# Softmax steps of a decoder layer: value products and sample pieces moved between the scores and the weights' transposes, on TensorE

## The reference

```python
def block(args):                       # i: one block of 128 queries
    i, qn, qr = args
    s = jnp.einsum('bqhn,bkhn->bhqk', qn, k_nope) + jnp.einsum('bqhp,bkp->bhqk', qr, kr)
    s = s.astype(F32) * MLA_SCALE
    s = jnp.where(key_pos[None, :] <= q_pos[:, None], s, -jnp.inf)
    p = jax.nn.softmax(s, axis=-1).astype(v.dtype)
    return jnp.einsum('bhqk,bkhv->bqhv', p, v)
...
# samples
q_lat = jnp.einsum('bshn,rhn->bshr', q_nope, w_uk)
state = jnp.exp(gt)[..., None] * state + kt[..., None] * vt[..., None, :]
```

## Time and profile before

| | us |
|---|---|
| median of 3 runs | 735.47 (734.77 to 735.70) |
| the profiled execution, its own time | 736.7 |
| its span in the trace | 734.9 |
| the stretch of steps 4 to 49 in it | 168 (from 388 to 556) |

### The profile page before, as it was taken

How to read it: one execution, slowest core, us unless ns; L and a number is a source line. 1 busy time by engine, 2 the same in 40 slices (tenths; PEclk the granted TensorE clock), 3 DMA queues, 4 the chain that set the end, 5 groups by cost and what they waited for, 6 DMA issues and landing times.

```text
span 734.9 us, 16715 instructions
## 1 busy us (share of the span) xinstructions
PE 700.0 (95%) x7021; PEld 549.6 (75%) x7021; DVE 355.9 (48%) x775; ACT 326.7 (44%) x779; POOL 91.1 (12%) x140
## 2 busy tenths in 40 slices
PE   2899999999999999899899999999999999999995
PEld 1487878878789997677667766777677998678884
DVE  0455370030202025777675676667671112389967
ACT  1244660021202137767556666645675667502100
POOL 0000000000000011101124323232113442000000
PEclk9899999999999999999999999999999999999998
DMA  9987300302001001000010000202756884203332
GB/s 289 395 351 214 112 3 1 114 1 76 22 1 58 1 29 58 16 10 16 9 12 2 1 2 0 59 1 74 243 187 214 293 290 150 61 1 117 135 123 86
DMA packets 35013, 70.31 MB, mean 96 GB/s; under 512 B 6594, under 2 KB 17947, under 8 KB 33020
## 3 DMA queue, kind: packets, MB, share of 16 engines
q1 hardware_dynamic: 30602, 47.73, 20.1%
q0 software_dynamic: 3728, 20.97, 8.1%
q10 hardware_dynamic: 610, 0.55, 0.3%
HBM read 62.26 MB, written 6.07 MB: 93 GB/s over the span
## 4 chain that ended last, share of the span: by engine, by line
PE 90%; DVE 3%; ACT 2%; issue 1%; DMA 1%; another core or an unknown queue 1%; ACTq 1%; DVEq 0%
PE banks L2051 21%; PE banks L2247 8%; PE banks L2063 6%; PE banks L2377 5%; PE banks L2461 4%; PE banks L2481 3%; PE banks L2590 3%; PE banks L2592 3%; PE banks L2591 3%; PE banks L2072 2%; PE banks L2530 2%; PE banks L2549 2%; PE banks L2155 2%; PE banks L2573 2%; PE banks L2574 2%; PE banks L2580 2%
## 5 line engine op out<-in xcount | busy, mean ns | idle before, releaser
L1122 ACT ACTIVATE s_z<-banks 128x512 f32<-128x512 f32 (+3 forms) x40 | 19.6, 500 | 129.0 <-PE banks L2051 129.0
L2051 PE MATMUL banks<-s_w_parts,s_h_b 128*128 128x272 f32 (+3 forms) x328 | 68.2, 323 | 0.0
L1334 ACT ACTIVATE s_z<-banks 128x512 f32<-128x512 f32 (+2 forms) x88 | 41.3, 518 | 45.6 <-PE banks L2461 44.5
L1497 DVE COPY s_zs<-banks 8x512 f32<-8x512 f32 (+3 forms) x6 | 3.5, 576 | 118.5 <-PE banks L2025 118.5
L2051 PEld LDWEIGHTS banks<-s_w_parts,s_h_b 128*128 128x128 f32 x328 | 49.3, 189 | 4.6 <-issue 1.7
L1325 ACT ACTIVATE s_z<-banks,s_temps 128x896 f32<-128x896 f32 (+7 forms) x64 | 47.1, 741 | 11.0 <-DVE s_temps L1775 8.0
L2051 PE MATMUL banks<-s_w_parts,s_h_a 128*128 128x256 f32 (+2 forms) x256 | 49.8, 314 | 0.0
L2051 PE MATMUL banks<-s_z_r,s_h_b 128*128 128x512 f32 (+1 forms) x152 | 48.8, 387 | 0.0
L2461 PEld LDWEIGHTS banks<-s_ident,s_z 128*128 128x128 f32 x288 | 33.2, 141 | 11.7 <-issue 5.5
L2461 PE MATMUL banks<-s_ident,s_z 128*128 128x128 f32 x288 | 40.0, 275 | 1.3 <-DVE s_z L1791 1.2
L2051 PE MATMUL banks<-s_z_r,s_h_a 128*128 128x512 f32 x128 | 40.9, 395 | 0.0
(11 more groups left out here) (427 smaller groups left out, 1544.6 us busy)
## 6 DMA issues: line engine op xcount, KB each, us to landing
s_z<-in_w_ada SPq DMA_DIRECT2D x16, 512.0 KB, 12.2
s_temps<-in_w_in SPq DMA_DIRECT2D x3, 2048.0 KB, 7.7
s_x<-in_x_prompt SPq DMA_DIRECT2D x8, 512.0 KB, 12.0
s_z<-in_w_ada SPq DMA_DIRECT2D x1, 4096.0 KB, 13.9
s_kt<-in_w_out SPq DMA_DIRECT2D x8, 512.0 KB
s_temps<-in_x_prompt SPq DMA_DIRECT2D x8, 512.0 KB
out_y_prompt<-s_temps SPq DMA_DIRECT2D x7, 512.0 KB
s_temps<-in_w_in SPq DMA_DIRECT2D x2, 832.0 KB, 14.2
```

The source lines that it names most:

```text
L1334: nc.scalar.activation(PTb[r % 3][:, 4 * g:4 * g + n, :], banks[:, 4 + (groups(r) + g) % 2, 0:P * n].rearrange("p (j q) -> p j q", j=n), A ...
L2051: last = nc.tensor.matmul(banks[:, proj_bank(c, t), 0:WIDTH[c]], h_[half][:, k, n0:n0 + P], w_, start=(k == 0 and n == 0), stop=(k == KT - ...
```

## The change

In PE's loop the products and TAIL's piece now stand in front of `weights_turned(r)`. A piece at HEAD stays where it was. TAIL's projections and transposes of queries stay behind the turning. The products that stood ahead of the turning in step 48 still do. No instruction is added or taken away, no wait is changed, and no other engine's stream differs.

```diff
                             if s == len(STEPS):
                                 products(N_PAIRS_OF_HEADS - 2)
-                            weights_turned(r)
                             for p in range(N_PAIRS_OF_HEADS - 2):
                                 if last_step(p) == r - 1:
                                     products(p)
+                            if piece_at(s, TAIL):
+                                piece((s, TAIL))
+                            weights_turned(r)
                     if (s, place) in PROJECTED_AT:
                         bank_of_queries((s, place))
                         q_proj(*PROJECTED_AT[s, place])
                     if (s, place) in TURNED_AT:
                         bank_of_queries((s, place))
                         q_transpose(*TURNED_AT[s, place])
-                    if piece_at(s, place):
-                        piece((s, place))
+                    if place == HEAD and piece_at(s, HEAD):
+                        piece((s, HEAD))
```

## The result

The changed kernel takes 738.81 us (median of 6 runs, 738.12 to 741.70), the kernel before 735.14 (6 runs, 732.44 to 737.11). The ratio over the runs is 1.0062, with a 95% interval of 1.0044 to 1.0080: slower by 3.2 to 5.9 us. The two medians by themselves stand 3.67 us, or 0.50%, apart. The forecast was 739.0 us, range 737.0 to 741.6.

What follows compares the result with a forecast made beforehand. The prediction took PE to bound steps 4 to 49 (busy 166.1 of 168 us). Costs of 6.7 us less gains of 1.8 and 1.4 made +3.5 on the median 735.47: 739.0 us, range 737.0 to 741.6.

Steps and rivals of the forecast that it cites:

- three takers of bank 7: Steps 14/15, 20/21 and 23/24: PE work needing bank 7 waits for ACT's later copy, +1.1 us each, 3.3 together.
- q0: Step 11: q0 waits for ACT's later copy of the transpose of queries, seven transposes come behind it, +1.3 us.
- qlat: Step 29: qlat waits for ACT's copy of a transpose of queries, held behind delayed exponentials, +0.5 us.
- P27: Step 44: these products wait for ACT's copies of turned weights, ready at 535.25, +0.8 us.
- others: o1, step 7's projection, P4, P22 and two short waits for exponentials: +0.8 us together, between 0 and 2.
- waits for the scaling: PE's standing for DVE's scaling ahead of the turning, to be covered by moved work: -1.8 us, 1.4 in step 22.
- passages: Changes between kinds of PE work get cheaper, some 18 steps and steps 9, 29, 32: -1.4 us, between -0.5 and -2.
- its version of the sum: By the skill's drain rule alone, the gain from passages would be 0.5 rather than 1.4 us, the sum 0.9 higher.
- (a): Rival: the cover works and ACT's chain doesn't reach PE; gains alone, -3.2 us, 732.3 us; 7%.
- (b): Rival: handovers cost half of what was counted, 6.7 becomes 3.3 and it cancels: 735.5 to 735.7 us; 8%.
- (c): Rival: new collisions of DVE with POOL, 1.2 us per hit where PE has no cover: 740 to 742.6 us; 17%.

Runs made afterwards that it cites:

- e4_change_again: The changed kernel run once more with no edit: median 739.75 us against 736.41, ratio to the kernel before 1.0033.
- e3_three_back: The changed kernel with the order of before put back in steps 14, 20 and 23 only; ratio to the kernel before 0.9998.
- e8_pool_held: The kernel before with one wait added on POOL, holding its 8x1024 copy until DVE has scaled step 20's weights; ratio 0.9987.
- e12_qlat_twice: The kernel before with the products of piece qlat computed twice (16 more instructions of 8 columns); ratio 1.0043.
- e2_act_copy_first: The changed kernel with ACT's copy that frees bank 7 taken ahead of the copies of turned weights and the exponentials; ratio to the kernel before 0.9982.
- e6_pieces_first: Against the kernel before, only the pieces at the end of a step moved ahead of the turning, products left behind it; ratio 1.0032.
- e5_chosen_steps: The changed kernel's order in 20 chosen steps only, the order of before elsewhere; 731.67 us against 735.07, ratio to the kernel before 0.9955.

## Why the prediction was right

The time (739.0 against 738.8) and the way it comes about are as forecast. That the time came within 0.2 us is luck: the runs of the changed kernel alone spread over 3.6 us, the loss reads 3.1 in the steps and 4.5 by the ratio, and by that of e4_change_again 2.4. What counts is that the sum of the terms missed by 0.45 us and each came near its size; these are read in the steps, without the spread between executions.

| term | forecast | measured | where |
|---|---|---|---|
| three takers of bank 7 | +3.3 | +2.93 | steps 16, 22, 25; gone in e3_three_back |
| q0 | +1.3 | +1.16 | step 12 |
| qlat | +0.5 | +0.5 | step 30: +0.32, with the pair of passages (0.20) that went in step 29 |
| P27 | +0.8 | +0.7 | step 45 |
| others | +0.8 | +1.2 | o1 0.54, P4 0.29, 0.19 at step 49, 0.11 at 34, 0.07 at 8 |
| waits for the scaling | -1.8 | -1.8 | steps 17, 23, 35, less a passage of 0.05 each |
| passages | -1.4 | -1.7 | 18 steps, 0.88; steps 10, 33 and 30, 0.60; what hides in others |
| sum | +3.5 | +3.05 | |

*The takers of bank 7* came out 0.1 us cheaper each, and step 20 shows why. The turning starts 2.01 us behind the last scores (445.23 to 447.24) where it was 0.43 (444.12 to 444.55 in before): the delay of 1.58 was right. But the slack on ACT was 0.58 and not 0.46: with nothing to wait for, the exponentials start 0.65 behind the start of the copies (447.93 to 448.58), 0.12 ahead of the recorded end of these, where they had started 1.23 behind (445.25 to 446.48). 1.58 - 0.58 = 1.00, which is what step 22 shows. I had read slack from the end of a record; the engine takes its next instruction a little before that.

*P27* was summed a little wrong: the copies ready at 535.25 and P27 able to start at 534.56 make 0.7, not the 0.8 that was written, and 0.68 is what the step shows.

*The others* were mis-sized in the other direction. o1 behind ACT's copy of o0 costs 0.54 us, and P4 stands 0.51 us for DVE's mix of P3 where it had stood behind the turning; I had given all five of them 0.8.

*The passages.* Scores directly ahead of products, not seen before, cost 0.09 as charged (445.23 to 445.75 in the changed kernel: 0.43 for the last scores and the passage). Scores behind the turning read 1.72 us throughout. The gain is 0.05 a step and 0.20 where a pair of passages goes, as written. The sum was a little larger than I took, well inside its bounds. The rule of the Trainium skill ("TensorEngine Tiling (Array Packing)", Tiling Modes) that a change of mode drains is borne out by 0.094 us at each passage into the products and out of them; but width alone doesn't tell what such a change is (wT0, 64 columns wide like the products, cost 0.094 behind them and nothing ahead of the turning). The re-entry differs by what comes next, which that rule alone wouldn't give, and its version of the sum (0.9 higher, +4.4) fits the 3.05 worse.

*The span.* I forecast a span of 738.4; it was 736.7. Of the 1.7 us, 0.45 is the sum above. Another 0.68 lies ahead of step 3 (383.94 to 383.27 us), and 0.56 behind the first transpose of step 49, both in code that is the same. This is the scatter of one execution, and no term of the sum. About three quarters of the scatter between runs (73% of its variance) go with the clock: over all runs of the study, with a level of its own for each kernel and chip, the time is 0.61 us (0.56 to 0.67) shorter for each 0.001 by which the mean granted clock is higher.

*The rivals.* (a), that ACT's chain doesn't reach PE, and (b), that half of it is caught up, are refuted by the waits, each near its size. (c), new collisions of DVE with POOL, happened without harm: the scalings at 450.33 took 1.36 us beside POOL's L974, but PE was in the transposes of queries and the scores meanwhile, and then in P12. e8_pool_held shows that my reading of the old collision gave one operation what two had done.

## What to carry to other kernels

Before work is moved ahead of a step that feeds another engine, ask what hangs on that engine's stream behind it: a copy that frees a shared buffer, put behind all else in a fixed order, turns every delay at its head into a standstill of the engine that was to be relieved. Either move the other engine's order along with it, or make the move only where nobody waits; here that turned +3 us into -3. Compare orders by the lag at the same instruction of two traces, which repeats to hundredths, before trusting medians that spread by microseconds.

## What the runs showed of the hardware

- PE pays 0.094 us for each passage from scores or transposes to the products of 64 columns and back, and transposes that follow such a passage or a standstill are 0.05 us longer (five of 0.71 against 0.77). None of it was paid between scores, transposes of weights and of queries. The width of the tile alone doesn't decide it: from the products to wT0, both 64 columns wide, it was paid (0.20 us from the last product's start to wT0's first in the kernel before, where the products' own pace is 0.10), and from wT0 to the scores it was not (0.11 us, its own pace).
- Two DVE scalings of 128x512 took 0.88 us alone, 1.37 beside one POOL product of 8x256 (0.72), and 2.13 beside that and a POOL copy of 8x1024 (1.11).
- Behind the products of 8 columns (sixteen, and thirty-two in e12_qlat_twice) the granted clock was 0.50 for about 3.4 us in four traces, and for 10 us in one, costing 1.6 to 4.7 us. It came with and without a standstill of 0.47 us ahead of them (e2_act_copy_first, e6_pieces_first), and both kinds also went by without it (the changed kernel, e5_chosen_steps). The long one, e6_pieces_first, where qlat starts at 478.39 (busy times by stretch, granted clock last but two):

```profile
480.00:481.00 1.00, 1.00 (x10) 0.88 (x9) 0.59 (x3) 0.00 (x0) 0.34 (x3) 1.00 0.00 0
481.00:482.00 1.00, 1.00 (x12) 0.93 (x12) 1.00 (x2) 0.90 (x3) 1.00 (x3) 0.52 0.00 0
...
488.00:490.00 2.00, 2.00 (x6) 1.70 (x6) 0.73 (x2) 1.47 (x4) 0.00 (x0) 0.50 0.00 0
490.00:491.00 1.00, 1.00 (x2) 0.34 (x1) 0.00 (x0) 0.10 (x1) 0.00 (x0) 0.50 0.00 0
491.00:492.00 1.00, 1.00 (x7) 0.83 (x6) 0.19 (x1) 0.00 (x0) 0.00 (x0) 0.86 0.00 0
```
